# The last four weight units in front of each norm and the first three behind it, taken in two halves of the tokens

## The reference

```
def layer_norm(x, g, b):
    mu = jnp.mean(xf, axis=-1, keepdims=True)
    var = jnp.mean(jnp.square(xf - mu), axis=-1, keepdims=True)
    y = (xf - mu) * lax.rsqrt(var + LN_EPS) * g + b

def rms_norm(x, g):
    y = x32 * lax.rsqrt(jnp.mean(x32 * x32, axis=-1, keepdims=True) + EPS)

x = layer_norm(DN_ALPHA * x + mix, ...)                    # norms 0 and 2
x = layer_norm(DN_ALPHA * x + sqrelu_mlp(x, ...), ...)     # norms 1 and 3
x = x + rms_norm(mixer(rms_norm(x)))                       # norms 4 and 6
x = x + rms_norm(ffn(rms_norm(x)))                         # norms 5 and 7
```

## Time and profile before

| what | us |
|---|---|
| median of 3 runs | 2588.27 (2586.74 to 2588.28) |
| the profiled execution | 2587.15 |
| its span, first to last instruction | 2585.3 |
| TensorE busy | 2504.3 (97%) |
| VectorE, ScalarE, GpSimd busy | 1390.5, 1038.1, 252.2 |
| mean granted TensorE clock | 0.99 of 2.4 GHz |

### The profile page before, as it was taken

One profiled execution on the slowest core, in us unless ns is written; L12 is line 12 of the kernel. 1 busy time (PEld: TensorE's weight loads), 2 busy tenths in 40 slices (PEclk: granted clock), 3 DMA queues, 4 the chain that ended last, 5 costly groups with the idle time before them and its releaser, 6 DMA issues.

```text
span 2585.3 us, 29676 instructions
## 1 busy us (share of the span) xinstructions
PE 2504.3 (97%) x12214; PEld 2011.7 (78%) x12214; DVE 1390.5 (54%) x1943; ACT 1038.1 (40%) x1690; POOL 252.2 (10%) x192
## 2 busy tenths in 40 slices
PE   8999999999999899999999999999999999999998
PEld 6768878888877678888867778888877777788886
DVE  5547755443356765334454457646465453676354
ACT  5533235332246544223244444433244554444331
POOL 0030121000031430000121001100000000110000
PEclk9989999999999999999999999999999999999999
DMA  5210012222213122222211122222222112232221
GB/s 197 89 34 1 2 65 82 98 98 98 98 50 114 65 82 98 98 98 98 98 63 58 41 82 98 98 98 98 84 80 75 33 50 66 69 111 97 99 86 45
DMA packets 55062, 206.35 MB, mean 80 GB/s; under 512 B 3552, under 2 KB 3600, under 8 KB 54800
## 3 DMA queue, kind: packets, MB, share of 16 engines
q1 hardware_dynamic: 54288, 201.34, 22.8%
q0 software_dynamic: 640, 3.12, 0.3%
HBM read 202.30 MB, written 2.10 MB: 79 GB/s over the span
## 4 chain that ended last, share of the span: by engine, by line
PE 85%; DVE 6%; issue 5%; ACT 3%; POOL 1%; DMA 0%; SPq 0%; DVEq 0%; POOLq 0%; ACTq 0%
PE ps L268 25%; PE ps L270 25%; PE ps L269 25%; DVE WL L248 1%; PE ps L317 1%; PE ps L2267 1%; PE ps L321 1%; PE ps L2296 1%; PE ps L318 1%; DVE AR L626 1%; DVE AR L1752 1%; PE ps L2280 1%; PE ps L684 1%; DVE X L519 1%; DVE TM L516 1%
## 5 line engine op out<-in xcount | busy, mean ns | idle before, releaser
L268 PE MATMUL ps<-XH,WH 128*128 128x512 f32 x1960 | 787.2, 402 | 43.5 <-DVE XL L613 11.8
L269 PE MATMUL ps<-XL,WH 128*128 128x512 f32 x1960 | 766.9, 391 | 0.0
L270 PE MATMUL ps<-XH,WL 128*128 128x512 f32 x1960 | 766.8, 391 | 0.0
L248 DVE TENSOR_TENSOR WL<-RAW,WH 128x1024 fp32r<-128x1024 f32 (+1 forms) x382 | 465.9, 1221 | 338.3 <-ACT WH L240 337.5
L240 ACT ACTIVATE WH<-RAW 128x1024 fp32r<-128x1024 f32 (+1 forms) x382 | 395.3, 1037 | 320.5 <-PE ps L270 313.1
L268 PEld LDWEIGHTS ps<-XH,WH 128*128 128x128 f32 x1960 | 370.1, 189 | 139.0 <-issue 41.6
L269 PEld LDWEIGHTS ps<-XL,WH 128*128 128x128 f32 x1960 | 370.2, 189 | 81.8 <-issue 7.9
L270 PEld LDWEIGHTS ps<-XH,WL 128*128 128x128 f32 x1960 | 370.1, 189 | 78.0
L268 PE MATMUL ps<-H,WH 128*128 128x512 f32 x960 | 380.9, 397 | 1.7 <-ACT AR L1660 1.7
L269 PE MATMUL ps<-H,WH 128*128 128x512 f32 x960 | 380.5, 396 | 0.0
L270 PE MATMUL ps<-H,WL 128*128 128x512 f32 x960 | 380.5, 396 | 0.0
(11 more groups left out here) (372 smaller groups left out, 2511.5 us busy)
## 6 DMA issues: line engine op xcount, KB each, us to landing
RAW<-in_w SPq DMA_DIRECT2D x64, 1024.0 KB, 4.8
RAW<-in_up SPq DMA_DIRECT2D x44, 1024.0 KB, 4.9
RAW<-in_dn SPq DMA_DIRECT2D x16, 1024.0 KB, 4.8
RAW<-in_hyb SPq DMA_DIRECT2D x10, 1024.0 KB, 6.1
RAW<-in_qkv SPq DMA_DIRECT2D x9, 1024.0 KB, 4.9
RAW<-in_rin SPq DMA_DIRECT2D x8, 1024.0 KB, 4.8
RAW<-in_kvf SPq DMA_DIRECT2D x8, 1024.0 KB, 5.2
RAW<-in_dn SPq DMA_DIRECT2D x8, 768.0 KB, 4.2
```

Source lines behind the costliest of these rows:

```text
L248: dve.e.tensor_tensor(WL[:, s, 0:n], RAW[:, g % NRAW, k, 0:n], f32(WH[:, s, 0:n]), ALU.subtract).then_inc(*w_lo.at(u))
L268: pe.e.matmul(out, wh, xh, start=first, stop=False)
L269: pe.e.matmul(out, wh, xl, start=False, stop=False)
L270: return pe.e.matmul(out, wl, xh, start=False, stop=last)
```

## The change

The last four units in front of every norm are done first for tokens 0 to 255, then again for 256 to 511 (`last_four_pe`), so every one of their matmuls becomes two of 256 columns with the same weight block. The same holds for the first three units behind norms 0 to 6 (`first_three_pe`). All statistics, norms and splits of XH and XL are done per half, on tiles 256 wide. The fillers (`busy`) are gone. The statistics matmuls of half 0 stand behind the first unit of the second half; those of half 1 stand, in norms 0 to 2, 4 and 6, behind the second block of the first three units' first half. While VectorE and ScalarE norm half 0 they also take the second-half tiles out of PSUM, square and add them, and split the next three weight units (`lead_dve`, `lead_act`). The squares of norms 3 to 6 are no longer summed on TensorE: VectorE (norm 3) or GpSimd (4 to 6) adds them into S1, and one matmul per half closes the sum.

```
-        def busy(pe, n):
-            for _ in range(n):
-                pe.e.matmul(PS[7][:, 0:128], ident, ident, start=True, stop=True)
...
+        def last_four_pe(pe, us, xh, xl, ready, taken, behind_first):
+            kb = PLAN[us[4]][2]
+            for v in range(2):
+                for b, u in enumerate(us[4:8]):
+                    claim(pe, b)
+                    pe.wait_ge(w_lo, u)
+                    for k in range(kb):
+                        pe.wait_ge(*ready[k])
+                        mm = three(pe, PS[b][:, HALF[v]], u, k, xh[k][:, HALF[v]], xl[k][:, HALF[v]], k == 0, k == kb - 1)
+                    mm.then_inc(*(unit_done if v else half_done).at(u))
+                    pe.until[b] = [taken(b + 4, v)]
+                    if v and b == 0:
+                        behind_first()
+
+        def first_three_pe(pe, us, stage, behind):
+            for v in range(2):
+                for k in range(8):
+                    for b, u in enumerate(us[:3]):
+                        if (v, k) == (0, 0):
+                            claim(pe, b)
+                            pe.wait_ge(w_lo, u)
+                        pe.wait_ge(x_lo, (stage, k) if v else (stage, k, 0))
+                        mm = three(pe, PS[b][:, HALF[v]], u, k, XHS[k][:, HALF[v]], XLS[k][:, HALF[v]], k == 0, k == 7)
+                        if (v, k) == (1, 7):
+                            mm.then_inc(*unit_done.at(u))
+                    behind(v, k)
...
-                pe.e.matmul(PS[6][:, :], onesd, TM[:, 6 + m % 2, :], start=m == 0, stop=m == 7).then_inc(*rs_sum.at((n, m)))
+        def square_pool(pool, key, m, v):
+            h = HALF[v]
+            pool.wait_ge(rs_sq, (key, m, v))
+            if m > 1:
+                pool.wait_ge(rs_sum, (key, m - 1, v))
+            pool.e.tensor_tensor(S1[:, h], S1[:, h], TM[:, 6 + m % 2, h], ALU.add).then_inc(*rs_sum.at((key, m, v)))
...
+        def lead_dve(dve, take, stat, u0):
+            def between(i):
+                if i in (2, 4, 6, 8) and take:
+                    take(3 + i // 2, 1)
+                if i in (4, 6, 8):
+                    stat(2 + i // 2, 1)
+                if i == 9:
+                    stat(7, 1)
+                if i in (5, 7, 9) and u0 < len(PLAN):
+                    split_lo(dve, u0 + (i - 3) // 2)
+            return between
+
+        def lead_act(act, take, stat, u0):
+            def between(m):
+                if m in (2, 4, 6, 7):
+                    j = 3 + m // 2 if m < 7 else 7
+                    if take:
+                        take(j, 1)
+                    stat(j, 1)
+                if m in (3, 5, 7) and u0 < len(PLAN):
+                    split_hi(act, u0 + (m - 1) // 2)
+            return between
...
+        def norm_dve(dve, n, take, u0):
+            stats_end_dve(dve, n, 0)
+            layer_norm_dve(dve, n, 0, lead_dve(dve, take, stat, u0))
...
+                stats_end_dve(dve, n, 1)
+            layer_norm_dve(dve, n, 1, nothing)
```

More of the change, by code:

```diff
@@ L488, in rms_apply_dve @@
+        X_FROM = {"qkv": [[(x_norm, (3, m, v)) for m in range(8)] for v in range(2)]}
+        def rms_apply_dve(dve, stage, gname, gi, r, v, between):
+            h = HALF[v]
             for i in range(10):
@@ new lines, in rms_add_dve, with rms_add_pool @@
+                    dve.e.scalar_tensor_tensor(t, Y[:, i, h], vec("ng", gi + i), RS[:, h], ALU.mult, ALU.mult).then_inc(*ln_c.at((n, "y", i, v)))
+                    if i not in ON_POOL[n]:
+                        dve.wait_ge(ln_c, (n, "y", i, v))
+                        dve.e.tensor_tensor(X[:, i, h], X[:, i, h], t, ALU.add).then_inc(*x_mix.at((("add", n), i, v)))
+                between(i)
+        def rms_add_pool(pool, n, v):
+            h = HALF[v]
+            for i in range(9):
+                if i in ON_POOL[n]:
+                    pool.wait_ge(ln_c, (n, "y", i, v))
+                    pool.e.tensor_tensor(X[:, i, h], X[:, i, h], TM[:, 3 + i % 3, h], ALU.add).then_inc(*ln_p.at((n, "add", i, v)))
+                if i > 1 and n < 7:
+                    square_pool(pool, n, i - 1, v)
@@ new lines, in mixed, with mix_out_pe @@
+        def mixed(key):
+            return lambda m, v: (x_mix, (key, *earlier(m, v)))
+        def mix_out_pe(pe, name, n, nk, ahead=None):
+            us, banks = UNIT[name], OUT_BANKS[name]
+            run(ahead or beside(pe, us[:3], banks, XHS[:nk], XLS[:nk], ready_of(name, nk)))
+            for i in range(4):
+                if i == 3:
+                    unit(pe, us[3], banks[3], XHS[:nk], XLS[:nk], ready_of(name, nk))
+                pe.until[banks[i]] = [mixed((name,))(i, None)]
+            last_four_pe(pe, us, XHS[:nk], XLS[:nk], ready_of(name, nk), mixed((name,)), lambda: stats_pe(pe, n, 0, True))
@@ L855, in mlp_pe @@
                 hh, hl = [H[:, o + k, :] for k in range(8)], [H[:, o + 8 + k, :] for k in range(8)]
-                for m in range(8):
+                ready = [(h_lo, (l, q, k)) for k in range(8)]
+                for m in range(8 if (what, q) != ("dn", 3) else 4):
                     if what == "up":
@@ L1082, in mix_y_dve @@
[L1082 to L1087 removed]
+            for i in range(4):
+                if i == 3:
+                    unit(pe, us[3], banks[3], xh[:nk], xl[:nk], ready_of(name, nk))
+                pe.until[banks[i]] = [(ev_act, us[i])]
+            last_four_pe(pe, us, xh[:nk], xl[:nk], ready_of(name, nk), y_there(name), lambda: stats_pe(pe, n, 0, False))
```

693 lines of the change are left out of this document (414 added, 279 removed).

## The result

| what | before | after |
|---|---|---|
| median, us | 2587.64 (2586.74 to 2588.28) | 2608.42 (2606.76 to 2610.05) |
| span of the profiled execution | 2585.3 | 2605.2 |
| mean granted clock | 0.990 | 0.969 |

The ratio is 1.0081, with a 95% interval of 1.0063 to 1.0098: slower by 20.8 us. The forecast was 2595 us and slower. The sign and most of the mechanism hold; the size is short by 13 us. The median lies inside the range (to 2609) by 0.6 us, two of the four executions (2609.85 and 2610.05) lie above it, and the forecast's own range (2591 to 2602) doesn't hold it. So the range was right by a hair.

A forecast was written before the change was run, and what follows sets the result against it. TensorE, busy 2504.3 of 2585.3 us, was taken as the bound. Norms 0 to 2 (+8.1), 4 (-0.1), 6 (-2.0), 3 (+2.8), 5 (+1.3) and 7 (-2.4) summed to +7.7 us: 2595 us, range 2576 to 2609.

The forecast's parts named there:

- The matmuls, +13 us: Product matmuls around the norms: 1200 pairs at 0.239 us for 0.228, +13 us; the skill's formula would give 3 us.
- Third WL at 22.5: Norms 0 to 2: the third unit's weight split ends 22.5 us after unit 7's first-half matmuls, holding TensorE back.
- With the clock 1.5 us; bounds 0 and 3: Behind each norm's gap: some three microseconds of TensorE at half rate cost 1.5 us, between 0 and 3.
- The fillers' removal itself is worth nothing: they lay in waits: Filler matmuls in the gaps at the norms: taking them out neither gains nor costs time by itself.
- Norms 4 and 6, 49.7 and 53.3: Last four to first three units: 49.7 us for 49.8 before (-0.1) and 53.3 for 55.3 (-2.0).
- Norm 5, 56.9: Stage at norm 5, two norms in succession, reckoned like norm 3: 56.9 us against 55.6 before, +1.3.
- norm 3, 66.5: Stage at norm 3, two norms in succession: 66.5 us against 63.7, +2.8; half 1's first XL at 44.9.
- Contention, 2.0 us per norm: Half 0's pass: VectorE operations waiting out GpSimd ones add 2.0 us, between 0 and 2.6.
- Squares off TensorE, -16 us: Norms 4 and 6: squares matmuls leave the product in the first three units, 2 x (24.4 - 16.4) = -16 us.
- Norm 7, -2.4: Last norm to the program's end: 33.1 us against 35.5 before, -2.4.
- 1: Rival 1: halves overlap as drawn, without GpSimd lock and with full clock: 2571, one alone 2581 to 2585; chance 0.27.
- 3: Rival 3: GpSimd's 256-wide operations stay near 1.3 us and bound both passes, 2605 to 2609; chance 0.10.

The follow-up runs named there:

- half_only: Kernel before, with 1200 of its 512-wide product matmuls issued as pairs of 256-wide ones and nothing else changed: 2598.02 us, ratio 1.0040.
- fourth_split: Changed kernel, with the fourth unit's splits at norms 4 and 6 moved into the pass of half 1: 2601.05 us, ratio 1.0050.
- gpsimd_off: Changed kernel, with the layer norms' multiply by RS (norms 0 to 3) moved from GpSimd to VectorE: 2605.74 us, ratio 1.0064.

## Why the prediction was right and wrong

- **The matmuls, +13 us: right within the noise.** half_only gives 10.2, for 504 of the 1200 pairs in other units; its interval (7.2 to 13.7) holds 13 and not 3. The 3 us came from the formula of the Trainium skill ("TensorE: Matmul & The Clock Gate", Back-to-back issue gap). That section gives it for an isolated matmul, and says that among weight loads it comes out too low for small N, so it was used outside its case; the trace disagrees with it here, 119 to 120 ns for its 109 and 228 for its 216.
- **Third WL at 22.5, "the weights aren't" in time: right for norms 0 to 2** (21.8 measured from the same zero at norm 0). How it was added up is only in part borne out: the sum queued the work on ScalarE, and the trace has ScalarE busy for 13.3 and VectorE for 14.6 of the pass's 17 us, with VectorE's idle time nearly all ahead of the first XL. What an early WL was worth was not asked: with the splits early, banks and then statistics are next, and only 1.2 to 2.2 us per layer norm come back.
- **"With the clock 1.5 us; bounds 0 and 3": too small.** In the row that I sized it from the earlier trace rows TensorE was busy from 341 on and the half level ended some 3 us later; here the 1.2 GHz level lasted ten microseconds at norm 0, six of them matmuls. Fillers in the same place gave back 2.6, 2.7 and 2.4 us at norms 0 to 2. This is the term of the sum that was mis-sized, by 1 us per norm: from the restart to the end of the first three units norms 0 to 2 took 20.1, 20.2 and 19.9 us for the 19.1 of the sum.
- **"The fillers' removal itself is worth nothing: they lay in waits": true of their length only.** They still held the clock, which the prediction says elsewhere and counts as the 1.5 us term; that term is their worth.
- **Norms 4 and 6, 49.7 and 53.3: each 1.5 to 1.8 short, and a term was missing.** Inside the stages the third WL came 0.8 and 0.5 us later than written, and what follows it took some 1 us more, as at norms 0 to 2. Behind them, the sum counted three splits of four. The fourth went from the start of the pass to behind its end. fourth_split measures it: 7.4 us in all, the largest single part of the 13 us that the forecast fell short. The prediction looked at what leads TensorE's first block and not at what had been queued behind it.
- **Norm 5, 56.9: 3.2 short; norm 3, 66.5: 0.8 too long.** At norm 5 half 1's first product came 49.3 us behind the stage's start and not 46.8, and the matmuls behind it took 0.6 us more than written; at norm 3 it came at 55.1 and not 56.4. So "in the same form" didn't carry over from norm 3 to 5. At norm 5 the squares matmul waits for GpSimd's adds (L553, 8.4 us); whether these are the cause was not tried.
- **Contention, 2.0 us per norm: seen in the operations, not shown on the path.** Without GpSimd's eight multiplies VectorE's other operations in half 0's pass are shorter by 2.3 us in sum, but putting the multiplies on VectorE fills the same time, and the pass stays as long. What GpSimd's operations cost the path by themselves no run shows.
- **Squares off TensorE, -16 us: only inside the whole.** Alone, at full width, it costs 9 us and gains none. In the changed kernel the holes between blocks are gone: from the third unit's restart to the last product matmul of the first three it is 20.2 us at norms 4 and 6, about as long as at norms 0 to 2 (19.9 to 20.2). What that is worth there isn't known from a run of its own.
- **Norm 7, -2.4: right** (33.2 for 33.1), in its total; its parts were not measured one by one.
- **Rivals.** 1 had its point of decision at clock 1.00 and a third WL before 20.5; neither came. 3 has the changed kernel's time (2605 to 2609) by another cause: GpSimd's multiplies took 0.83 us at norm 0, and TensorE has no wait inside half 1 of norms 0 to 2.

One rest was not tried: the stretch from norm 1 to norm 2 is some 2 us longer. In it TensorE waits for an XL tile in the LRU mixer (L2000) for 13.5 us, 11.2 before, and behind it the clock is at half for some 6 us of matmuls, some 3 before.

## What to carry to other kernels

Before a phase is split to overlap it, add up what the helper engines must do in the window: here VectorE had next to no room behind its first tile, so the idle time of TensorE mostly changed its place, and the halved matmuls (8.5 ns per pair, 1200 pairs) came on top. When a schedule is rewritten, follow the last item of every queue that moved, not just the first one that the bound engine needs; one split left behind cost 3.7 us at each of its two norms, and getting three late ones early gave at most 2.9 per norm. When a run comes out as its theory says, look whether the gain lies where the theory put it: GpSimd's multiplies had the right sign, and it was the clock. And look first for work on the bound engine that can be done in fewer passes where it stands: that gave 10 and then 4 us, at the price of the low parts of the sums.

## What the runs showed of the hardware

- A 512-wide fp32 matmul between product matmuls took 0.87 us of TensorE's time (2.92 less nine at 0.228), the fp32r one 0.24. A 128-wide fp32 filler took 0.23, with two records in the profile.
- GpSimd's 512-wide add took 1.69 us beside a busy VectorE and 1.30 elsewhere, and VectorE's own add 1.27 us for 0.69. More work on GpSimd was paid for on VectorE. With 256-wide multiplies on GpSimd the WL split took 1.53 us, without them 1.21.
- A filler of no use to the model kept the clock at 1.00 where the same gap without it had left six microseconds of matmuls at the 1.2 GHz level (0.213 us from one 256-wide matmul to the next, for 0.12).
- Behind the same 34 us to the restart at norm 0, the half level covered nearly 6 us of matmuls in the changed kernel and some 3 in gpsimd_off. So a change of 1 us in a stage can be the clock's.
